# Gathering four slots of 32 tokens instead of one slot of 128, and summing with 32 stationary columns

## The reference, cut to what matters

```
# h: normalised tokens (256 x 1024); w_q, sub_keys: choose, per token and per head
# (8 heads), 16 of 16384 rows; gate: softmax of the 16 scores
def block(args):                       # 128 tokens at a time
    xt, et, gt = args                  # tokens, expert ids (128,8,16), gates
    act = gelu(einsum('td,thkd->thk', xt, u[et]), approximate=False)
    return einsum('thk,thkd->td', act * gt, v[et])
```

## Time and profile before

| | |
|---|---|
| median of 3 runs | 3061.08 us (3058.69 to 3063.8) |
| profiled execution | 3065.34 us, of which the span is 3063.6 |
| TensorE products | busy 2502.5 us, 82% |
| VectorE | 1370.5 us, 45% |
| ScalarE | 860.6 us, 28% |
| GpSimd | 580.8 us, 19% |
| gathers (software queue) | 536.90 MB, 42.3% of 16 engines' span |
| plain loads | 558.26 MB, 43.6% |

### The profile page before, as it was taken

One profiled execution on the slowest core, in us unless ns is written; L12 is line 12 of the kernel. 1 busy time (PEld: TensorE's weight loads), 2 busy tenths in 40 slices (PEclk: granted clock), 3 DMA queues, 4 the chain that ended last, 5 costly groups with the idle time before them and its releaser, 6 DMA issues.

```text
span 3063.6 us, 31433 instructions
## 1 busy us (share of the span) xinstructions
PE 2502.5 (82%) x10904; PEld 1302.0 (42%) x10904; DVE 1370.5 (45%) x3289; ACT 860.6 (28%) x2283; POOL 580.8 (19%) x558
## 2 busy tenths in 40 slices
PE   8999855657999965667798987798987989977777
PEld 6776311113777421213455632264452645422222
DVE  1352100002143201000366667778657786677774
ACT  0131100000122100000233334457434584343343
POOL 0000000000000000000013444423334243444442
PEclk9999887778999988888899999999999999999999
DMA  7237999999344799999716999999999999999997
GB/s 310 114 117 290 396 429 428 428 428 427 145 170 168 309 428 427 428 428 428 322 59 253 422 421 421 421 422 422 420 421 421 409 405 413 421 421 422 421 419 310
DMA packets 121197, 1100.30 MB, mean 359 GB/s; under 512 B 13488, under 2 KB 17360, under 8 KB 21968
## 3 DMA queue, kind: packets, MB, share of 16 engines
q1 hardware_dynamic: 45584, 558.26, 43.6%
q0 software_dynamic: 73728, 536.90, 42.3%
q10 hardware_dynamic: 1728, 3.14, 0.3%
HBM read 1094.06 MB, written 4.19 MB: 358 GB/s over the span
## 4 chain that ended last, share of the span: by engine, by line
DMA 44%; PE 42%; DVE 7%; issue 3%; ACT 3%; POOL 1%; SPq 0%; DVEq 0%; ACTq 0%
PE ps L670 22%; DMA wbuf<-in_puv,ar 21%; PE ps L1332 9%; DMA wbuf<-in_w_expert_down 8%; DMA wbuf<-in_w_expert_up 8%; DMA wbuf<-in_w_expert_gate 5%; PE ps L981 3%; DVE ar L2086 3%; DMA wbuf<-in_w_mem_kv 2%; PE ps L825 2%; PE ps L674 2%; ACT ar L2149 1%; PE ps L770 1%; PE ps L793 1%; DVE ar L1361 1%
## 5 line engine op out<-in xcount | busy, mean ns | idle before, releaser
L1332 PE MATMUL ps<-wbuf,ar 128*128 128x512 f32 x2048 | 967.0, 611 | 216.5 <-ACT ar L2149 216.3
L2086 DVE CUSTOM_DVE_ANT_0 ar<-wbuf,Y 128x1024 f32<-128x1024 f32 x512 | 628.5, 1227 | 331.2 <-DMA wbuf<-in_puv,ar 318.0
L2669 POOL DMA_INDIRECT wbuf<-in_puv,ar x512 | 556.3, 1087 | 860.1 <-PE ps L1332 737.0
L1332 PEld LDWEIGHTS ps<-wbuf,ar 128*128 128x128 f32 x2048 | 369.1, 192 | 764.7 <-issue 762.8
L981 PE MATMUL ps<-wbuf,ar 128*32 128x512 f32 x2944 | 458.4, 760 | 284.1 <-DMA wbuf<-in_w_expert_up 111.6
L2149 ACT ACTIVATE ar<-ar 128x1 f32<-128x1 f32 (+1 forms) x1053 | 270.3, 257 | 662.9 <-DVE ar L2086 633.2
L670 PE MATMUL ps<-HT,wbuf 128*128 128x256 f32 (+1 forms) x2496 | 438.7, 334 | 5.1 <-DMA wbuf<-in_w_mem_kv 5.1
L670 PEld LDWEIGHTS ps<-HT,wbuf 128*128 128x128 f32 x2496 | 385.1, 192 | 57.3 <-issue 11.3
L981 PEld LDWEIGHTS ps<-wbuf,ar 128*32 128x32 f32 x2944 | 93.1, 125 | 631.0 <-issue 213.9
L2653 POOL TENSOR_TENSOR sm<-sm,co 128x1 f32<-128x1 f32 (+1 forms) x18 | 10.1, 563 | 1560.2 <-DVE sm L1367 1560.0
L1358 DVE COPY ar<-ps 128x512 f32<-128x512 f32 (+5 forms) x89 | 55.4, 623 | 411.5 <-PE ps L981 273.0
(11 more groups left out here) (169 smaller groups left out, 1637.6 us busy)
## 6 DMA issues: line engine op xcount, KB each, us to landing
wbuf<-in_w_expert_down SPq DMA_DIRECT2D x64, 2048.0 KB, 32.2
wbuf<-in_w_expert_up SPq DMA_DIRECT2D x62, 2048.0 KB, 30.6
wbuf<-in_w_expert_gate SPq DMA_DIRECT2D x58, 2048.0 KB, 30.8
wbuf<-in_w_in SPq DMA_DIRECT2D x22, 2048.0 KB, 19.0
wbuf<-in_peer_w_q SPq DMA_DIRECT2D x12, 2048.0 KB, 11.6
wbuf<-in_w_o SPq DMA_DIRECT2D x6, 2048.0 KB, 11.8
wbuf<-in_b_w_in SPq DMA_DIRECT2D x6, 2048.0 KB, 11.6
wbuf<-in_w_branch_b SPq DMA_DIRECT2D x4, 2048.0 KB, 16.4
```

The source lines that it names most:

```text
L1332: m = T.e.matmul(acc[n][:, :], DG[:, j % 4, :], rows_of(name)[:, 1024 + 512 * n:1536 + 512 * n], start=(j == 0), stop=(j == 127))
L2086: V.did(V.e.tensor_tensor_reduce(JK, rows_of(f"g{l}{i}.{j}")[:, 0:1024], Y[:, i, :], 1.0, 0.0, ALU.mult, ALU.add, DT[:, i, j:j + 1]), f"do ...
L2669: G.land(G.e.indirect_dma_start(out=rows_of(name), out_offset=None, in_=I["puv"], in_offset=bass.IndirectOffsetOnAxis(ap=IX[:, i, j:j + 1] ...
```

## The change

A gather now holds four slots of 32 tokens. With g the block of 32 tokens, partition 32k + t receives slot 4b + k of token 32g + t, so a set of 32 slots is again 32 gathers: 4 blocks g times 8 values of b. What follows from it:
- The token's values must stand four times, one below the other: `copies` makes them with products of a 32-column slice of the identity (8 TensorE jobs per stage into PSUM), and VectorE and ScalarE copy them to a weight tile. That tile was the fifth pair of gather buffers: the ring has 8 buffers now. Copies for the next stage are made near the end of a stage, one block when its last gather is through.
- Addresses and gates come from `route` with a token per partition and have to be spread the same way: `spread` does it with products of 4 or 8 moving columns, and VectorE copies from PSUM to `IX` and to `GP`, the new table of gates.
- The diagonal becomes `quad`, four 32 x 32 identities one below the other, so the stationary operand has 32 columns and sums the four slots. The 32 output rows of half n stand in column group (g + 2n) mod 4, so the second half's PSUM bank holds its blocks two groups further on. At the end of a stage ScalarE's `swapped` copies it back in order, to Y, and `collect` adds that.
- In each set of 32 gathers, three places take a second step of `route`, which has two to three steps more.

```
-            rows_landed = [sem(f"rows_landed{k}") for k in range(10)]
+            rows_landed = [sem(f"rows_landed{k}") for k in range(8)]
...
+        GATHERS = [(q, g, b) for q in range(4) for g in range(4) for b in range(8)]
+        FIRST = [(0, g, b) for h in range(2) for g in range(4) for b in range(4 * h, 4 * h + 4)]
...
+            def copies(l, i, g):
+                T.wait_ge(*at[READY[l, i]])
+                for h in range(2):
+                    job = f"yr{l}{i}.{g}{h}"
+                    b = take(job)
+                    for k in range(4):
+                        m = T.e.matmul(b[32 * k:32 * k + 32, :], ident[:, 32 * g:32 * g + 32],
+                                       Y[:, i, 512 * h:512 * h + 512], start=True, stop=True, tile_position=(0, 32 * k))
+                    T.did(m, job)
+
+            def spread(job, *srcs):
+                b, c = take(job), 0
+                for src in srcs:
+                    v = four(src)
+                    n = v.shape[1]
+                    for g in range(4):
+                        for k in range(4):
+                            m = T.e.matmul(b[32 * k:32 * k + 32, c + n * g:c + n * g + n], ident[:, 32 * g:32 * g + 32],
+                                           v[:, :, k], start=True, stop=True, tile_position=(0, 32 * k))
+                    c += 4 * n
+                T.did(m, job)
...                                                  # prep_both, TensorE
-                drain(route(0, 0, 0))
+                next(route(0, 0, 0))
+                for g in range(4):
+                    copies(0, 0, g)
                 out_product(0, 1, (3, 4, 5))
+                spread_index(0)
                 out_product(1, 1, (6, 7, 0, 1, 2, 3, 4, 5))
                 for k in range(2):
                     raw("p0", 1, k, f"ma.r{k}1.out")
+                spread_gates(0)
...                                                  # route, TensorE
-                for _ in range(13):
-                    yield
+                for _ in range(14):
+                    yield
+                T.wait_ge(*at[p + ".gt"])
+                spread(p + ".pm", I12[:, 0].rearrange("p h n -> p (h n)"), GA[:, i, 32 * q:32 * q + 32])
+                yield
...                                                  # stage, TensorE
-                            if j % 4 and not rate:
+                            if j % 32 in (0, 16, 20):
                                 next(nxt, None)
...
                         for n in range(2):
-                            m = T.e.matmul(acc[n][:, :], DG[:, j % 4, :], rows_of(name)[:, 1024 + 512 * n:1536 + 512 * n],
-                                           start=(j == 0), stop=(j == 127))
+                            o = 32 * ((g + 2 * n) % 4)
+                            m = T.e.matmul(acc[n][o:o + 32, :], DG[:, j % 4, :], rows_of(name)[:, 1024 + 512 * n:1536 + 512 * n],
+                                           start=(g not in begun), stop=(j == last_of(g)), tile_position=(0, o))
...                                                  # prep_both, VectorE
                 drain(route_head(0))
+                head_spread("i", 0)
                 add(0, 1)
                 add(1, 1)
                 mean_a("p0", 1)
                 mean_b("p0", 1)
                 scaled("p0", 1)
                 head_gates(0)
+                head_spread("g", 0)
...                                                  # head_spread(kind, h)
+                job = f"rt000.p{kind}{h}"
+                V.wait_ge(*at[job])
+                src = ps(job)[:, 0:16].rearrange("p (g b) -> p g b", g=4)
...                                                  # collect, VectorE
-                for n in range(2):
-                    xs = half_of(X, i, n)
-                    tt(xs, xs, ps(f"acc{l}{i}.{n}")[:, :], ALU.add, f"acc{l}{i}.{n}.out")
+                xs = half_of(X, i, 0)
+                tt(xs, xs, ps(f"acc{l}{i}.0")[:, :], ALU.add, f"acc{l}{i}.0.out")
+                V.wait_ge(*at[f"acc{l}{i}.sw"])
+                xs = half_of(X, i, 1)
+                tt(xs, xs, half_of(Y, i, 0), ALU.add, f"acc{l}{i}.1.out")
...                                                  # stage, VectorE
-                        V.did(V.e.tensor_tensor_reduce(JK, rows_of(f"g{l}{i}.{j}")[:, 0:1024], Y[:, i, :], 1.0, 0.0,
-                                                       ALU.mult, ALU.add, DT[:, i, j:j + 1]), f"dot{l}{i}.{j}")
+                        V.did(V.e.tensor_tensor_reduce(JK, rows_of(f"g{l}{i}.{j}")[:, 0:1024], copies_of(g), 1.0, 0.0,
+                                                       ALU.mult, ALU.add, DT[:, i, c:c + 1]), f"dot{l}{i}.{j}")
...                                                  # ScalarE
+            def swapped(l, i):
+                A.wait_ge(*at[f"dm{l}{i}.127"])
+                for k in range(2):
+                    copy(Y[64 * k:64 * k + 64, i, 0:512], ps(f"acc{l}{i}.1")[64 - 64 * k:128 - 64 * k, :],
+                         *([f"acc{l}{i}.sw"] if k else []))
...
-                        act(DG[:, j % 4, :], ident, ACT.Copy, f"dg{l}{i}.{j}", scale=d)
+                        act(DG[:, j % 4, :], C("quad"), ACT.Copy, f"dg{l}{i}.{j}", scale=d)
...                                                  # GpSimd
-            count, rows = {}, Ring(10)
+            count, rows = {}, Ring(8)
```

More of the change, by code:

```diff
@@ L621, in sync_program @@
             row("row.ffn20", "ffn20")
-            before_rows = ("ma.w0", "ma.uk", "ma.uv", "ma.wo0", "ma.wo1")
+            before_rows = ("ma.uk", "ma.uv", "ma.wo0", "ma.wo1")
             shape["row_tiles"] = [shape[name][0] for name in before_rows]
-            shape["rows"] = [before_rows[k // 2] for k in range(10)]
-            for k in shape["row_tiles"]:
+            shape["rows"] = [before_rows[k // 2] for k in range(8)]
+            shape["copies"] = shape["ma.w0"][0]
+            for k in (*shape["row_tiles"], shape["copies"]):
                 tiles.keep(k)
@@ L1310, in second_head @@
                     yield
+                spread_index(1)
+                yield
+                for n in range(4):
+                    if n == 1:
+                        spread_gates(1)
+                    next(nxt)
+                    next(nxt)
+                    yield
                 yield from nxt
             def stage(l, i, after, side, rate):
+                begun, coming = set(), COMING.get((l, i))
                 acc = [take(f"acc{l}{i}.{n}", keep=True) for n in range(2)]
@@ L2412, in prep_both @@
                 next(steps)
+                for g in range(2):
+                    for h in range(2):
+                        copied(0, 0, g, h)
                 head_exp(0)
+                for g in range(2, 4):
+                    for h in range(2):
+                        copied(0, 0, g, h)
                 for half in range(2):
```

98 lines of the change are left out of this document (83 added, 15 removed).

## The result

The changed kernel took 3071.74 us (median of 6 runs, 3068.27 to 3076.91) beside 3060.86 us of the kernel before (6 runs, 3058.69 to 3065.11): ratio 1.0035, 95% interval 1.0022 to 1.0048, so 6.7 to 14.7 us more, 10.9 in the middle. The profiled execution took 3071.74 us, of which the span is 3069.8. Forecast: 3068.5.

The account below looks back on a forecast made before the run. The retrieval layers were taken as DMA-bound by their gathers. Head +7.8, middle 0 and tail -0.4 made +7.4 us, so 3068.5 us on the median; the forecast's own range 3065 to 3073, with A, E and half of C 3059 to 3078.

Parts of the forecast that it names:

- Part 4: Head: the second add waits for `ma.r11` behind the address spread, delaying the stream from gather 1; +7.8 us, bounds +6.5 to +9.8.
- Part 1: Gather products two side by side: 437 us less TensorE work under the DMA; worth 0 to 6.5 us in the middle.
- Part 2: Ring of 8 instead of 10 where the queue runs low: taken as 0, with 5 us kept upward for 2470:2545.
- Part 3: Token copies and spreads added beside the stream: 0 with part 2 and what part 1 gives back; bounds -6 to +5 us.
- Part 5: Tail: last products -0.86 us, diagonal -0.11, second add waiting for ScalarE's swap +0.55; sum -0.4 us.
- A: Rival: TensorE's relief counts in 2380:2640, both weak stretches reaching 421 GB/s; 3061 us, chance 0.15.
- B: Rival: the order of the rows makes the gather transfers faster, 428 GB/s; 3047 us, chance 0.05.
- C: Rival: ring of 8 starves where VectorE is over 88% busy and in the first 50 us; 3080 us, chance 0.12.
- D: Rival: column groups don't overlap in the head's copies, TensorE reaching the spread 18 us late; 3086 us, chance 0.03.
- E: Rival: the change hides in the head because VectorE's add isn't late; 3063 us, chance 0.10.

Follow-up runs that it names:

- paced kernel: Changed kernel with the route inside the side work of layer 1's stages given the same three double steps as the others; 3072.13 us, ratio 1.0035.
- run with the root later: Changed kernel with GpSimd's root of tile 1 issued after gather 7 instead of after gather 0; 3071.51 us, ratio 1.0035.
- reordered head: Changed kernel: TensorE does `ma.r11` and block 0's copies before both spreads, VectorE gates before tile 1's adds, ScalarE's other copies later; 3067.45 us, ratio 1.0018.
- narrow products alone: Kernel before with gather products of 32 stationary columns in two column groups, sums of 96 tokens left out, ring of 10; 3061.37 us, ratio 1.0002.
- output product first: Changed kernel with the eight products of `ma.r11` ahead of the spread of the first addresses on TensorE; 3071.27 us, ratio 1.0034.
- two reordered heads with the root later: Reordered head with GpSimd's root after gather 2 instead of gather 0: 3072.98 us, ratio 1.0035; with layer 1's route steps also doubled: 3072.37, 1.0032.
- three variants: Kernel before with a ring of 8 (3063.54 us), with narrow products (3061.37), or with the root behind gather 1 instead of gather 0 (3062.23).
- the same with the copies later: Reordered head with ScalarE's four copies of blocks 2 and 3 moved behind the second and fourth diagonal; 3070.31 us, ratio 1.0026.

## Why the prediction was right, step by step

The forecast of +7.4 us stands beside 10.9 measured (6.7 to 14.7), 12.2 by the marker. Direction, place and chain were right, and so was the link that was priced. A second limit close behind it was not seen, and the middle was not free. By the traces the 12.2 us are 8.7 up to gather 127 (forecast 7.8), 3.4 behind it up to the tail (forecast 0) and 0.1 in the tail (forecast -0.4). One of the prediction's readings is off and nothing hangs on it: VectorE is busy up to 92% of a stretch (36.85 of 40 us in 1660:1700), not 89%.

**Part 4, the head.** Microseconds after the marker:

| step | before | forecast | after |
|---|---|---|---|
| addresses back on VectorE | - | 1.6 | 0.6 |
| `ma.r11` done | ahead of it | 8.5 | 9.3 |
| second add done | 1.7 | 9.5 | 10.1 |
| gather 1 issued | 3.8 | 11.6 | 12.1 |
| first dot product | 7.4 | 15.7 | 16.6 |
| first product on TensorE | 11.1 | none given | 20.3 |

The spread took 0.43 us where 1.5 was allowed, and `ma.r11` 8.8 us for 16 instructions where 6.9 was: it ran partly at the lower clock (granted 0.83 in 1630 to 1640), which fell right behind an idle stretch of 1.86 us and the spread. Its first four instructions stand 0.85 to 0.96 us apart, the others 0.43, which makes 1.8 us. That the two errors, -1.1 and +1.9 us, all but cancel is luck.

The main step held: "The stream from gather 1 on is 7.8 us later, and since it is DMA-bound to the end nothing takes that back". It landed 8.1 us later and gather 127 8.7. What the prediction had wrong is what stands next to it: "The gates and the first dot, with one more spread and a copy ahead of them, come at about 1652, before gather 1 can land", and so "hide behind it". They come with it, not clearly before it: in the changed kernel the second dot product follows the first without a wait, in its second profile it waits 0.49 us for its gather, in the paced kernel 0.24. The chain of gates, first dot product, table load and first diagonal holds the first product, that holds the first free buffers, and a ring of eight gives the DMA only 8 x 2.49 = 20 us of its own. So this chain is a second limit, some 2 us behind the first, and the run with the root later met it.

That the inversion on TensorE is behind the loss the reordered head shows: first dot product back at 7.7 us, gather 127 5.8 us sooner, and the median 4.7 us over before instead of 10.9 (the two intervals just overlap). Of the 2.9 us that still lack there at gather 127, 1.9 are gather 1's, behind a root that starts 5.0 us after the marker instead of 2.9. The other 1.0 arise at the ring's end, where ScalarE's chain holds the first product.

**Part 1, the products.** Worth 0 in the middle, as taken. The narrow products alone agree, within -1.8 to +3.4 us. The size of the saving was off (270 us, not 437), because the granted clock fell; in the middle nothing depended on it. The diagonal took 321 ns (0.29 forecast).

**Part 2, the ring.** Taken as 0; by itself 0.8 us (-1.5 to +4.0). But "a group's addresses come after gather 23 of 32 instead of 25" did not hold at the entries of layer 1's stages, whose route runs inside `prep_tile` with no steps doubled: there GpSimd's wait went from 6.42 to 11.16 us, and the share under 1.0 (0.74 in 2355:2365). Pacing it repaired the place and not the time.

**Part 3, beside the stream.** Taken as 0. First product to end took 1415.8 to 1419.5 us over the nine profiles of changed kernels (mean 1418.4) and 1416.1 to 1418.0 over the five of before (mean 1417.0): +1.4, for the changed kernel itself +3. Counted from gather 127 to the end it is 1.3 to 4.8 us more than before, 3.6 in the changed kernel; the ring of 8 alone has 1.5 of it in its one profile. This is the term of the sum that was mis-sized, and its cause isn't settled: ring, entries and spreads each fit, and none alone was seen to give it back.

**Part 5, the tail.** +0.1 instead of -0.4: the last products ran in part at 1.2 GHz.

**The rivals.** A fell: the weak stretch at 2380:2470 did come up to 422 GB/s, and 2090:2160 went down. B fell: 421 to 423 GB/s where the share is full, the rate of the earlier trace rows. C fell as a whole, with the ring's 1.5 us and the 11-us waits as its true part. D fell: 64 copies in 7.07 us. E fell: VectorE did wait 7.82 us.

**What stays open.** The output product first, and the two reordered heads with the root later, are 3 to 4 us shorter from marker to end than the changed kernel, yet their medians are within 1.3 us of it. Of all the edits to the changed kernel only the reordered head moves the median clearly. Median less marker to end is 1632.2 to 1633.4 in the four rows of the table with the spread of addresses ahead of `ma.r11`, 1635.6 to 1637.8 in the five with `ma.r11` first, and 1633.6 to 1634.7 in the kernel before and its three variants. The edited calls come too late in the program to move the marker itself, and one profile each can't tell whether the rest is chance. So the head's 8 us rest on the traces, on the forecast's own chain in them and on the one median of the reordered head. No version tried beats the kernel before. ScalarE's gained parts of tile 1 behind its first diagonals, together with an earlier root, were not tried.

## What to carry to other kernels

When a stream is fed through a ring, its start has two limits: when the first transfers are issued, and when the first buffers come free. Follow each moved step through to both, over every engine in between; the later one sets the stream, and closing its gap pays only down to the other. Here a root moved seven gathers down issued gather 1 nine microseconds sooner and won 2.6 us of the stream. Work taken off an engine that is not the limit buys nothing in the middle of the stream; what the new arrangement puts ahead of the stream is paid in full (8.1 us at gather 1, 8.7 at gather 127).

## What the runs showed of the hardware

**Less work, lower clock.** With the products two side by side TensorE's granted clock in 2640:3040 went from 1.00 to 0.73, and to 0.70 with the narrow products alone. At 1.05 us a gather, the row at 2.4 GHz, the 512 would take 538 us; they took 696.5.

**The spread's price.** 32 instructions of 4 columns, four groups side by side, took 0.43 us, 13 ns each. In the trace they start in sets of four, one set every 32 ns, and the last one alone lasts 0.17 of the 0.43 us. The Trainium skill, TensorEngine Tiling (Array Packing), Instruction Overhead, gives about 60 cycles for each product, from which the prediction made 32 x 25 ns = 0.8 us. Counted once for each set of four, an estimate from the same figure, it is 8 x 25 ns = 0.2 us; the measured starts, 8 x 32 ns = 0.25 us, agree with this count and not with the first.

**A late release.** In both profiles of the changed kernel and in that of the paced one the gate spread's last product ends at about 13.8 us after the marker and VectorE starts 2.6 us later; the profile names no releaser ("remote"). With the output product first it is 2.5 us. In the run with the root later, where GpSimd issued nothing at that moment, VectorE followed at once:

```profile
1642.72 0.17 DVE L1441 COPY ar<-ps 128x16 f32<-128x16 f32 x1 [0.64 <-PE ps L1176]
```

There the first dot product came 14.4 us after the marker instead of 16.6, and the first product 18.7 instead of 20.3: some 2 of the first product's 9.2 us. Whether GpSimd's issuing has to do with it is open: in the reordered head and in the same with the copies later GpSimd had begun gather 0 at the same 1.7 us after the marker when the gate spread ended at 2.0, and VectorE followed 0.1 us behind in the one and 1.2 in the other. What holds the release is not shown.
